# Modulation chunks spread over mixers and passages, and the down chunks' low parts on VectorE

## The reference

```
mod = silu(c) @ w_ada[l] + b_ada[l]            # 1024 -> 6 x 1024, one row for all tokens
sh_m, sc_m, gt_m, sh_f, sc_f, gt_f = split(mod, 6)
h = rms_norm(x, g) * (1 + sc_m) + sh_m         # layers 0, 1;  layers 2, 3: h = x * (1 + sc_m) + sh_m
y = mixer(h)
x = x + gt_m * rms_norm(y, g_post)             # layers 2, 3: x = layer_norm(alpha * x + (1 + gt_m) * y)
h = ... sc_f, sh_f in the same way
y = (gelu(conv(h @ w_up_act)) * (h @ w_up_lin)) @ w_down     # layers 0, 1, inner width 2816
y = (silu(h @ w_gate) * (h @ w_up)) @ w_down                 # layer 2, inner width 3584
y = top-2 mixture of 8 such experts                          # layer 3
x = x + gt_f * ...                             # as above
```

## Time and profile before

| | us |
|---|---|
| three runs | 2938.6, 2940.91 (median), 2950.54 |
| profiled execution | 2939.21 |
| its span, first to last instruction | 2937.4 |
| TensorE busy | 2647.3 (90%) |
| VectorE busy | 1749.4 (60%) |
| ScalarE busy | 1257.9 (43%) |
| GpSimd busy | 865.4 (29%) |
| DMA | 693.8 MB, 236 GB/s over the span |

### The profile page before, as it was taken

How to read it: one execution, slowest core, us unless ns; L and a number is a source line. 1 busy time by engine, 2 the same in 40 slices (tenths; PEclk the granted TensorE clock), 3 DMA queues, 4 the chain that set the end, 5 groups by cost and what they waited for, 6 DMA issues and landing times. The chain is left out here.

```text
span 2937.4 us, 36572 instructions
## 1 busy us (share of the span) xinstructions
PE 2647.3 (90%) x14371; PEld 2140.4 (73%) x14371; DVE 1749.4 (60%) x1950; ACT 1257.9 (43%) x1292; POOL 865.4 (29%) x389
## 2 busy tenths in 40 slices
PE   5997998997999876899987669999999999999996
PEld 4774887884888645688864547888888788887884
DVE  1243455434456495446439538777777777777776
ACT  1133333223333103233300216776767667777763
POOL 0000122000477170378227012222223223232222
PEclk8988999988999886899988679999999999999998
DMA  9732887331798310498731019999999999999993
GB/s 321 251 129 64 295 284 243 122 101 58 243 299 269 115 58 20 165 286 272 263 128 58 15 62 332 344 357 331 369 332 350 350 335 364 333 360 339 350 350 132
DMA packets 434952, 693.80 MB, mean 236 GB/s; under 512 B 37690, under 2 KB 255894, under 8 KB 434838
## 3 DMA queue, kind: packets, MB, share of 16 engines
q1 hardware_dynamic: 407456, 677.09, 66.4%
q10 hardware_dynamic: 27382, 15.10, 1.8%
HBM read 691.10 MB, written 1.05 MB: 236 GB/s over the span
## 5 line engine op out<-in xcount | busy, mean ns | idle before, releaser
L1240 ACT ACTIVATE region_part<-ring 128x2048 fp32r<-128x2048 f32 x432 | 806.0, 1908 | 287.4 <-DMA ring<-in_w_down 100.4
L697 PE MATMUL bank<-ring_part,region_part 128*128 128x512 f32 x1648 | 649.2, 394 | 0.0
L2003 DVE TENSOR_TENSOR ring_part<-ring,region_part 128x2048 fp32r<-128x2048 f32 x270 | 640.5, 2405 | 1.7 <-ACT region_part L1240 1.7
L695 PE MATMUL bank<-region_part 128*128 128x512 f32 x1432 | 582.6, 407 | 8.9 <-DVE ring_part L2003 6.2
L696 PE MATMUL bank<-region_part 128*128 128x512 f32 x1296 | 511.7, 395 | 0.0
L1133 POOL TENSOR_TENSOR ring_part<-ring,region_part 128x2048 fp32r<-128x2048 f32 x54 | 268.7, 4984 | 554.5 <-ACT region_part L1240 554.5
L1711 DVE TENSOR_TENSOR ring_part<-ring,region_part 128x2048 fp32r<-128x2048 f32 x72 | 206.0, 2881 | 279.4 <-ACT region_part L1240 279.4
L697 PEld LDWEIGHTS bank<-ring_part,region_part 128*128 128x128 f32 x1648 | 310.1, 188 | 71.5
L695 PE MATMUL bank<-xn_part,region_part 128*128 128x256 f32 x1152 | 329.0, 286 | 25.4 <-DVE hT_part L2041 10.5
L695 PEld LDWEIGHTS bank<-region_part 128*128 128x128 f32 x1432 | 269.8, 188 | 81.9 <-issue 17.5
L697 PE MATMUL bank<-hT_part,region_part 128*128 128x256 f32 x1152 | 327.3, 284 | 0.0
(11 more groups left out here) (287 smaller groups left out, 3656.8 us busy)
## 6 DMA issues: line engine op xcount, KB each, us to landing
ring<-in_moe_w_gate SPq DMA_DIRECT2D x126, 1024.0 KB, 5.0
ring<-in_moe_w_up SPq DMA_DIRECT2D x126, 1024.0 KB, 5.1
ring<-in_moe_w_down SPq DMA_DIRECT2D x126, 1024.0 KB, 4.8
ring<-in_w_ada SPq DMA_DIRECT2D x48, 1024.0 KB, 7.0
ring<-in_mod_w SPq DMA_DIRECT2D x48, 1024.0 KB, 5.3
ring<-in_w_in SPq DMA_DIRECT2D x44, 1024.0 KB, 5.5
ring<-in_w_up_act SPq DMA_DIRECT2D x22, 1024.0 KB, 7.2
ring<-in_w_up_lin SPq DMA_DIRECT2D x22, 1024.0 KB, 7.2
```

The costliest lines, as they stand in the source:

```text
L695: nc.tensor.matmul(o, split(a_hi), split(b_hi), start=start, stop=False, skip_group_check=True)
L697: return nc.tensor.matmul(o, split(a_hi), split(b_lo), start=False, stop=stop, skip_group_check=True)
L1240: return nc.scalar.activation(out_, in_, func, **kw).then_inc(*done(*event))
L2003: v.tensor_tensor(split(w), w, whole(hi), ALU.subtract).then_inc(*done("moe_lo", j, e))
```

## The change

Of the 24 modulation chunks of layer l + 1, 14 go into layer l's mixer, 4 behind its output projection, and 6 stay in its FFN stage, one in each of the first six groups. In layers 0 and 1 the 14 are summed in the units of the attention, in layer 2 in the units of the scan and around the glu matmuls. They add up in PSUM bank 5; `acc_out` copies them to `mod_acc` at the mixer's end, and the other ten, in bank 3, are added to that in group 5 of the FFN stage. Columns follow in group 7 and the gate halves in groups 8 to 11. Those of layer 0 itself go into units 1 and 5 of its attention. Several sets of banks become smaller by one to make room. In the FFN stages VectorE instead of GpSimd makes the low part of the down chunk, after the hidden activations of its group; GpSimd keeps the tables alone.

```diff
+ADA_MIX = 14
+ADA_PASS = 4
+ADA_BANK = 5
@@ def ada_in_ffn
-    n = ffn_groups(l) - 1
-    return list(range(ADA * g // n, ADA * (g + 1) // n)) if g < n else []
+    q = ADA_MIX + ADA_PASS + g
+    return [q] if q < ADA else []
@@ def chunk_plan
+            for q in range(ADA_MIX):
+                plan.append((("ada", l + 1, q), ("pe_used", "ada", l + 1, q)))
...
         for n in range(4):
             plan.append((("out", l, n), ("pe_used", "out", l, n)))
         if l == LAYERS - 1:
             break
+        for q in range(ADA_MIX, ADA_MIX + ADA_PASS):
+            plan.append((("ada", l + 1, q), ("pe_used", "ada", l + 1, q)))
@@ TensorE, norm_tiles
-        tiles = [bank(..., range(4))
+        free = (0, 1, 2, 4) if stage == "ffn" else (0, 1, 2, 3)
+        tiles = [bank(..., (free[b],))
@@ TensorE, attention
+                if l:
+                    pe.wait_ge(*until("c_second"))
+                ada_bank(l + 1, "mix", ADA_BANK)
...
                         m.then_inc(*done("pe_tile", "sc", l, u))
+                    ada_sum(l + 1, "mix", u, 0)
+                    if l == 0 and u == 1:
+                        mod_columns(0, 1, range(5))
+                        gate_half(0, 0, range(5))
+                        gate_half(0, 1, range(5))
+                    if l == 0 and u == 5:
+                        gate_half(0, 2, range(5))
+                        gate_half(0, 3, range(5))
@@ TensorE, ffn
-                ada_bank(l + 1, 1, 3)
                 for g in range(groups + 1):
                     if g < groups:
                         up(g)
                         for q in ada_in_ffn(l, g):
-                            ada_sum(l + 1, 1, q, 0)
-                    else:
-                        mod_columns(l + 1, 1, [3])
-                        gate_half(l + 1, 0, up_banks)
+                            ada_sum(l + 1, "rest", q, ADA_MIX)
+                    if g == 7:
+                        mod_columns(l + 1, "rest", (3,))
+                    if 8 <= g < 12:
+                        gate_half(l + 1, g - 8, (3,))
                     if g:
                         down(g - 1)
@@ TensorE, mixer_two, in the loop over the scan's units
                     if u < 8:
                         s5_in(u)
+                    if l == 2:
+                        ada_sum(3, "mix", u - 2, 0)
                     s5_out(u - 2)
+                for q in (8, 9):
+                    if l == 2:
+                        ada_sum(3, "mix", q, 0)
...
+                for q in range(10, ADA_MIX):
+                    if l == 2:
+                        ada_sum(3, "mix", q, 0)
@@ TensorE, main order
-                        elif i < 3:
-                            gate_half(l, 1 + i)
...
                 out_projection(l)
-                if l == 0:
-                    for h in (2, 3):
-                        gate_half(0, h, range(4))
+                if l < 3:
+                    ada_bank(l + 1, "rest", 3)
+                    for q in range(ADA_MIX, ADA_MIX + ADA_PASS):
+                        ada_sum(l + 1, "rest", q, ADA_MIX)
@@ GpSimd, ffn
                 for g in range(ffn_groups(l)):
-                    key = ("down", l, 0, g)
-                    pool.wait_ge(*until("w_hi", *key))
-                    nc.gpsimd.tensor_tensor(split(chunk(key)), chunk(key), whole(hi_part(key)), ALU.subtract).then_inc(*done("w_lo_down", l, g))
@@ VectorE, ffn
+                    key = ("down", l, 0, g)
+                    dve.wait_ge(*until("w_hi", *key))
+                    v.tensor_tensor(split(chunk(key)), chunk(key), whole(hi_part(key)), ALU.subtract).then_inc(*done("w_lo_down", l, g))
+                    if g == 5:
+                        acc_out(l + 1, "rest", ADA - 1)
+                        pick_gate(l + 1, 0)
+                        pick_gate(l + 1, 1)
+                    if g == 7:
+                        columns_out(l + 1, "rest", 0, ADA)
+                    if 8 <= g < 11:
+                        gate_out(l + 1, g - 8)
+                        if g < 10:
+                            pick_gate(l + 1, g - 6)
+                gate_out(l + 1, 3)
@@ VectorE, main order
-                if l:
-                    gate_out(l, 1)
-                    pick_gate(l, 3)
-                    gate_out(l, 2)
-                    gate_out(l, 3)
```

More of the change, by code:

```diff
@@ L551, in norm_tiles @@
                 src = xn if l < 2 else x
-                tiles = [bank(("norm", l, stage, b), ("hT", l, stage, b) if b % 2 == 0 else ("hTd", l, stage, b), range(4))
+                free = (0, 1, 2, 4) if stage == "ffn" else (0, 1, 2, 3)
+                tiles = [bank(("norm", l, stage, b), ("hT", l, stage, b) if b % 2 == 0 else ("hTd", l, stage, b), (free[b],))
                          for b in range(4)]
@@ L650, in attention @@
                         transposes(("pT", l, u - 1), ("att_pT", l, u - 1),
-                                   [(i * P, att_p[:, (u - 1) % 2, i * P:(i + 1) * P]) for i in range(4)], range(6))
+                                   [(i * P, att_p[:, (u - 1) % 2, i * P:(i + 1) * P]) for i in range(4)], range(5))
                     if u >= 2:
@@ L675, in o_transposes @@
                                [(i * S + t * P, xn[:, t, (2 * b + i) * P:(2 * b + i + 1) * P])
-                                for i in range(2) for t in range(NT)])
+                                for i in range(2) for t in range(NT)], range(4))
             def out_projection(l):
@@ L744, in ffn @@
                 groups = ffn_groups(l)
-                ada_bank(l + 1, 1, 3)
-                if l == 1:
-                    pe.wait_ge(*until("c_second"))
                 for g in range(groups + 1):
@@ L761, in mixer_two @@
                 hT_ready(l, "mix")
-                for i, n in enumerate((8, 0, 1, 2, 3)):
+                among = range(6)
+                if l == 2:
+                    among = range(5)
+                    usable[0] = (0, 1, 2, 3, 4, 6, 7)
+                    ada_bank(3, "mix", ADA_BANK)
+                for n in (8, 0, 1, 2, 3):
                     in_features(l, n)
-                    if i < 3:
-                        gate_half(l, 1 + i)
                 pe.wait_ge(*until("b_masked", l))
@@ L782, in s5_in @@
                     for r in range(2):
-                        o = bank(("bu", l, u, r), ("s5_w", l, u), range(6))
+                        o = bank(("bu", l, u, r), ("s5_w", l, u), among)
                         for jj in range(2):
@@ L820, in mixer_two @@
                         w = chunk(key)
-                        o = bank(key, ("in_out", l, n), range(6)).rearrange("p (t n) -> p t n", t=NT)
+                        o = bank(key, ("in_out", l, n), among).rearrange("p (t n) -> p t n", t=NT)
                         for t in range(NT):
@@ L1011, in _ @@
                     attention(l)
-                    if l == 0:
-                        mod_columns(0, 1, range(4))
-                        for h in range(2):
-                            gate_half(0, h, range(4))
                     o_transposes(l)
@@ L1109, in ffn @@
                     table_start(l + 1)
-                steps = list(TABLE_STEPS) if l else []
+                if l == 0:
+                    return
+                steps = list(TABLE_STEPS)
                 for g in range(ffn_groups(l)):
-                    key = ("down", l, 0, g)
-                    pool.wait_ge(*until("w_hi", *key))
-                    nc.gpsimd.tensor_tensor(split(chunk(key)), chunk(key), whole(hi_part(key)), ALU.subtract).then_inc(*done("w_lo_down", l, g))
                     if g == 0 and l == 2:
@@ L1654, in acc_out @@
                 dve.wait_ge(*until("pe_used", "ada", l, last))
-                v.tensor_copy(mod_acc, psum[bank_of["ada", l, part]][:, 0:CW]).then_inc(*done("mod_acc", l, part))
+                o = psum[bank_of["ada", l, part]][:, 0:CW]
+                if part == "rest":
+                    v.tensor_tensor(mod_acc, o, mod_acc, ALU.add).then_inc(*done("mod_acc", l, part))
+                else:
+                    v.tensor_copy(mod_acc, o).then_inc(*done("mod_acc", l, part))
             def columns_out(l, part, q0, q1):
@@ L1804, in attention @@
                         v.tensor_reduce(att_nm[:, u, 0:nh], s, AX.X, ALU.max, negate=True).then_inc(*done("att_max", l, u))
+                        if l == 0 and u == 1:
+                            columns_out(0, 1, 12, 20)
+                            gate_out(0, 0)
+                            gate_out(0, 1)
+                            pick_gate(0, 2)
+                            pick_gate(0, 3)
+                        if l == 0 and u == 5:
+                            gate_out(0, 2)
+                            gate_out(0, 3)
                     if 1 <= u <= n_units:
@@ L2287, in gla @@
                     after()
+                if l == 2:
+                    acc_out(3, "mix", ADA_MIX - 1)
             def route():
```

33 lines of the change are left out of this document (12 added, 21 removed).

## The result

The changed kernel takes 2870.03 us (median of four runs, 2869.58 to 2871.81), the kernel before, on the same chip, 2942.55: ratio 0.9751 (95% interval 0.973 to 0.9773). Forecast were 2892 us and a range that begins at 2870. The direction and the FFN stages' terms held; the gain in the profiles was 20 us larger than forecast, most of it in the attentions and the mixers. The profiled execution took 2869.81 us, its span 2868.0, and its mean granted clock is 0.943 where before it was 0.927.

A forecast was written before the change was run, and what follows sets the result against it. TensorE's instruction stream was taken to bound the FFN groups, with stalls from late weights. FFN stages -54, gates -8, passages -1, attention +12 and scan +2 gave -49 us: 2890, or 2892 on the median's footing; range 2870 to 2922.

The forecast's parts named there:

- the attention's price: First two attentions: fourteen chunks each, clock rising within the first units; +7 us in layer 0, +5 in layer 1.
- A term put at nothing: Behind layer 0's attention: moving the gates away saves nothing, as the normalised heads need those four us anyway.
- The mixers: Next three mixers: three gate halves leave each start, -8 us in all; chunks in layer 2's scan cost +2.
- The FFN stages: Three dense FFN stages: 204.8, 204.8 and 251.7 us rebuilt from pitches, 61 us saved; -54 after the tables' wait.
- GpSimd's bunched tables: First five or six FFN groups of layers 1 and 2: 0.5 to 1 us of wait a group, 7 in all.
- The low parts on VectorE: FFN groups: one more VectorE operation of 2.29 us each, costed at nothing; uncovered up to 2.3 us a group.
- The passages: Between output projection and FFN stage: layer 0 gains 4.7 us, layers 1 and 2 lose 2 each; net -1.
- The low clock (1): First half of both attentions: clock stays low, +37 us instead of +12, time 2917; chance 0.20.
- the stalls that stay (4): FFN stages: stalls stay, being high-part buffer latency, not DMA; 16 us less gained, 2908; chance 0.13.
- VectorE as the bound (3): Every FFN group: the new low part delays all behind it; +112 us on -49, time 3004; chance 0.04.
- GpSimd's tables (2): FFN stages: bunched tables block VectorE by the port lock; ten groups lose 2 to 3 us, 2910 to 2915; chance 0.10.
- The "better" case (5): Whole kernel: stalls, lower clock at the starts and attention all end well, about 2874 us; chance 0.08.

The follow-up runs named there:

- e_fill: Kernel before, with filler matmuls of a chunk's shape, without DMA, behind the scores of each attention's first two units: 2929.07 us, ratio 0.9951.
- e_late: Changed kernel with no modulation chunk in the attentions' first two units; units 2 and 3 sum two each: 2878.19 us, ratio 0.9774.
- e_pool5: Changed kernel with GpSimd making the down chunks' low parts as before, five rounds: 2875.62 us, against 2870.84 for the changed kernel on the same chip.
- e_dve: Kernel before, with VectorE instead of GpSimd making the down chunks' low parts, modulation chunks unmoved: 2933.87 us, ratio 0.9962.

## Why the prediction was off, step by step

**The step that failed** is the attention's price, "I take it that the clock rises within the first units in layer 0", with "+7" and "+5" for it. I took the low level of the earlier trace rows as given and asked what would end it. Where it began I didn't ask: in both attentions in TensorE's wait of 2.70 us for the first exponentials. With a chunk in each of the first two units the clock never falls there, and every unit costs 3.5 us instead of 4.64, the chunk included. Measured are +5.0 and -2.7, together +2.3 where I had +12. e_fill shows that matmuls in the first two units do this without any other part of the change, and e_late that without chunks there the time comes near my forecast: its attention and output projection 1 are 3.8 us above the kernel before, for my +5. This is 9.7 of the 20 us.

**A term put at nothing** lies inside these figures: "The four us that the gates fill today after the attention are needed there anyway". With the gates gone from there TensorE stands still for these 4.0 us, the clock falls at 228.65, and the transposes and the start of output projection 0 run at 1.2 GHz:

```profile
229.97 3.67 PE L531 MATMUL bank<-ident_sb,xn 128*128 128x128 f32 x16 [4.00 <-DVE xn L1871]
```

The projection takes 29.9 us instead of 27.7, which is 2.1 of the +5.0. In layer 1 it is the other way round: the same wait was there before, the low level lasted until 693.61, and the projection took 29.4 us; now the level is back after 3.4 us, and it takes 27.7, which is 1.7 of the -2.7. Why it comes back sooner there than in layer 0 or in e_late, no run shows; this part was luck. The attentions by themselves are at +2.9 and -1.0.

**The mixers** are some 6 us more. With three gate halves gone mixers 1 and 3 are 3.9 and 3.3 us shorter where I priced them at 2.7 each; what the other 1.2 and 0.6 us are, I have not traced. In layer 2 the chunks of the scan were to cost 2 us. They cost nothing in sum: counted from the end of FFN stage 1, the scan's first output matmul comes 3.2 us earlier than in the kernel before, the glu matmuls behind the loop 3.7, and the output projection 4.7. The kernel before had this wait of TensorE for a PSUM bank ahead of that first output, and the changed kernel has none of it:

```profile
PE bank L786 <- DVE region L2175: 3.9, 1, 3.9
```

Which of the changed sets of banks took it away, I haven't tested.

**The FFN stages** are right: 204.2, 207.3 and 250.7 us against 204.8, 204.8 and 251.7 from the pitches, plus 7 for GpSimd's bunched tables. Of these 7, only layer 1 shows some 2.5; that is the other 4.8 us. TensorE's waits for `hf_part`, 2.8 and 5.8 us in layers 0 and 1, are gone, as I had read the earlier trace rows. e_pool5 doesn't have them in layers 0 and 1 either, and e_dve still has them, so this is the moved chunks' doing and not VectorE's. That it is the chunks' DMA, and not something else of them, is my reading; no run separates the two.

**The low parts on VectorE** cost nothing, as forecast, and by e_pool5 they save about 5 us net. I had put their gain at nothing by itself and their side effect at +7; of that side effect layer 1 shows 1.8 us (207.3 against e_pool5's 205.5), and the gain outweighs it.

**The passages** are right to 0.4 us each: -4.6, +2.3 and +2.4 for -4.7, +2 and +2. ScalarE gets the second up chunk late, VectorE's low part follows, and the moments start 3.7 us after the squares began (697.25 is the gate's product, which stands before them), where the earlier trace rows have 1.4:

```profile
692.91 1.91 ACT L1273 ACTIVATE region_part<-ring 128x2048 fp32r<-128x2048 f32 x1 [4.99 <-DMA ring<-in_w_up_lin]
...
694.73 0.58 ACT L1273 ACTIVATE ffn_tmp<-bank 128x512 f32<-128x512 f32 x1
694.85 2.29 DVE L1748 TENSOR_TENSOR ring_part<-ring,region_part 128x2048 fp32r<-128x2048 f32 x1 [4.61 <-ACT region_part L1273]
...
697.25 1.22 DVE L1880 TENSOR_TENSOR mod_gate<-mod_gate,rows 128x1024 f32<-128x1024 f32 x1
...
698.40 0.15 DVE L1884 TENSOR_TENSOR stat<-stat 128x1 f32<-128x1 f32 x1
```

**The rivals.** The low clock (1) and the stalls that stay (4) did not come. VectorE as the bound (3) neither: no wait of TensorE for a low part on VectorE is in the lists. GpSimd's tables (2) show in one place. In layer 1's first group each of VectorE's operations is stretched beside them, 2.13 us for the two casts that take 0.49 at 388.78, 2.46 for 0.76, 3.16 for 2.29. GpSimd is held up as well: one operation of a table step, 1.04 us when alone, takes 3.12 beside the last of these. The second up block starts at 733.15, and TensorE has waited 5.73 us where layer 0's wait is 3.3:

```profile
729.63 2.13 DVE L2113 CAST prow_part<-hf 128x256 fp32r<-128x256 f32 x2
731.80 2.46 DVE L2116 TENSOR_TENSOR hf_part<-hf,prow_part 128x256 fp32r<-128x256 f32 x2
734.18 3.16 DVE L2119 TENSOR_TENSOR ring_part<-ring,region_part 128x2048 fp32r<-128x2048 f32 x1
735.16 3.12 POOL L1130 TENSOR_TENSOR region<-region 128x512 f32<-128x512 f32 x1
```

In these rows each of the two ends about its own free time after the other has ended. The mechanism is the lock's that the Trainium skill (SBUF — State Buffer, on the shared port pair) describes, and these rows agree with it. But it decides only where no down block covers VectorE, once a stage; in all later groups of layer 1 TensorE waits for nothing until the gate at the end. The "better" case (5), 2874 at a chance of 0.08, is what came, 4 us below it: I had the good ends of the terms, and gave them too small a chance together.

## What to carry to other kernels

Where a stretch runs at the lower clock, look for what came just before it fell, not only for what would lift it: a microsecond or two of work put there can be worth more than the work costs. The other side of it: a wait that looks free to empty, because the engine must wait there anyway, may cost the clock of what follows. Rebuild a stage from the pitches of its blocks; that was right to 1 us in two of three stages here. In a ring of slots, count for each chunk from its request to its use, since one that is asked for early holds its slot all that time, and the price falls on the chunks behind it.

## What the runs showed of the hardware

- Two sets of matmuls of 1.0 us each in the first two units made one attention 7.7 and the other 9.5 us shorter (e_fill). In the kernel before the level was at 1.2 GHz for 23.9 us (178.19 to 202.09, and 635.58 to 659.47), from within a wait of 2.70 us on, although TensorE was never idle in the five units that followed: scores of 64 rows, 128x128 transposes and products of 64 columns. In the changed kernel the same units with a chunk each run at 2.4 GHz throughout.
- The clock can fall while TensorE is busy: in e_late it fell at 178.17, during the gate matmuls, behind a wait of 0.89 us and 16 short scores, and was back at 181.58.
- In e_late's second attention the 1.2 GHz level ended at 621.90, while two chunks in a row ran (3.06 us from 619.55).
- A wait of 4.0 us before the transposes of layer 0's attention brought the level down for 10.2 us and made the output projection 2.1 us longer; the same wait in layer 1 brought it down for 3.4 us.
- Idle matmuls in waits of a passage raised its clock from 0.75 to 0.93 and took about 2.2 and 1.5 us from the two up blocks behind it. With those before the other stages and behind all three, the whole gain was 8.5 us.
- VectorE and GpSimd stretched each other: two casts took 2.13 us instead of 0.49, a low part 3.16 instead of 2.29, and one GpSimd operation of a table step, 1.04 us when alone, between 1.07 and 1.32 us beside the short VectorE operations and 3.12 beside a low part.
